# Input scaled by its inverse root once, banks emptied by ScalarE, and the keys of two heads in one unit, with the odd head's rotary product first

## What the kernel computes

```python
u = rms_norm_2(h, norm_mix_g[l])
proj = u @ w_in[l]
conv_in, c_q, c_kv, k_rope_raw, gate_logits = jnp.split(proj, cut, axis=-1)
conv_out = conformer_conv(conv_in, ...)      # a * sigmoid(gt), 31 taps, layer norm, silu, projection
mla_out = mla_attention(c_q, c_kv, ...)      # norms of both latents, 8 heads, causal softmax
gates = jax.nn.sigmoid(gate_logits).reshape(B, S, N_BRANCH, D_MODEL)
merged = gates[:, :, 0] * conv_out + gates[:, :, 1] * mla_out
h = h + merged @ w_out[l]
```

## Time and profile before

| | us |
|---|---|
| median of 3 runs (lowest to highest) | 2503.06 (2503.04 to 2503.13) |
| the profiled execution | 2503.1 |
| its span, first to last instruction | 2501.3 |
| TensorE busy | 2486.5 (99%) |
| VectorE busy | 1988.3 (79%) |
| ScalarE busy | 1244.2 (50%) |
| GpSimd busy | 305.2 (12%) |

### The profile page before, as it was taken

How to read it: one execution, slowest core, us unless ns; L and a number is a source line. 1 busy time by engine, 2 the same in 40 slices (tenths; PEclk the granted TensorE clock), 3 DMA queues, 4 the chain that set the end, 5 groups by cost and what they waited for, 6 DMA issues and landing times.

```text
span 2501.3 us, 36450 instructions
## 1 busy us (share of the span) xinstructions
PE 2486.5 (99%) x14212; PEld 2185.6 (87%) x14212; DVE 1988.3 (79%) x2830; ACT 1244.2 (50%) x1975; POOL 305.2 (12%) x250
## 2 busy tenths in 40 slices
PE   8999999999999999999999999999999999999998
PEld 7999988889999889999888899998888888888887
DVE  7878867778888688887777888876899786788873
ACT  6444444444444454444554544445577535654552
POOL 4000001220000000000023100000187221200002
PEclk9999999999999999999999999999999999999999
DMA  5333332233333323334323233334333333233331
GB/s 157 99 96 99 102 104 85 78 89 98 102 101 109 110 84 100 104 97 122 99 63 93 80 104 97 110 105 136 84 75 79 126 93 110 84 108 105 101 100 59
DMA packets 487297, 246.83 MB, mean 99 GB/s; under 512 B 42321, under 2 KB 483926, under 8 KB 486870
## 3 DMA queue, kind: packets, MB, share of 16 engines
q1 hardware_dynamic: 486674, 244.19, 33.9%
q10 hardware_dynamic: 452, 0.32, 0.0%
HBM read 240.27 MB, written 4.19 MB: 98 GB/s over the span
## 4 chain that ended last, share of the span: by engine, by line
PE 97%; DVE 1%; ACT 1%; DMA 0%; issue 0%; DVEq 0%; ACTq 0%
PE bank L893 8%; PE bank L892 8%; PE bank L891 8%; PE bank L774 6%; PE bank L775 6%; PE bank L776 6%; PE psS L913 5%; PE psS L914 4%; PE psS L915 4%; PE bank L1452 3%; PE psT L957 2%; PE psT L959 2%; PE psT L958 2%; PE psT L774 2%; PE psT L775 2%; PE psT L776 2%
## 5 line engine op out<-in xcount | busy, mean ns | idle before, releaser
L2267 DVE TENSOR_TENSOR wlo<-raw,whi 128x1024 fp32r<-128x1024 f32 (+2 forms) x212 | 288.8, 1364 | 49.8 <-ACT whi L1582 46.0
L774 PE MATMUL bank<-xhl,whi 128*128 128x512 f32 x672 | 264.5, 394 | 0.0
L775 PE MATMUL bank<-xhl,whi 128*128 128x512 f32 x672 | 261.9, 390 | 0.0
L776 PE MATMUL bank<-xhl,wlo 128*128 128x512 f32 x672 | 261.8, 390 | 0.0
L891 PE MATMUL bank<-xshl,whi 128*128 128x256 f32 x840 | 237.8, 283 | 0.0
L892 PE MATMUL bank<-xshl,whi 128*128 128x256 f32 x840 | 237.7, 283 | 0.0
L893 PE MATMUL bank<-xshl,wlo 128*128 128x256 f32 x840 | 237.7, 283 | 0.0
L1582 ACT ACTIVATE whi<-raw 128x1024 fp32r<-128x1024 f32 (+2 forms) x209 | 214.5, 1029 | 37.3 <-PE bank L776 22.2
L2330 DVE TENSOR_TENSOR wlo<-tw,whi 128x1024 fp32r<-128x1024 f32 x140 | 171.5, 1225 | 63.6 <-ACT whi L1622 63.5
L913 PE MATMUL psS<-hhi,whi 128*128 128x512 f32 x488 | 191.7, 393 | 0.0
L914 PE MATMUL psS<-hlo,whi 128*128 128x512 f32 x488 | 191.6, 393 | 0.0
(11 more groups left out here) (703 smaller groups left out, 7092.2 us busy)
## 6 DMA issues: line engine op xcount, KB each, us to landing
raw<-in_ffn_wg SPq DMA_DIRECT2D x88, 512.0 KB
raw<-in_ffn_wu SPq DMA_DIRECT2D x88, 512.0 KB
raw<-in_w_in SPq DMA_DIRECT2D x53, 512.0 KB
raw<-in_w_mlp SPq DMA_DIRECT2D x40, 512.0 KB
raw<-in_ffn_wd SPq DMA_DIRECT2D x48, 256.0 KB
raw<-in_ffn_wd SPq DMA_DIRECT2D x24, 448.0 KB
raw<-in_ffn_wd SPq DMA_DIRECT2D x48, 192.0 KB
raw<-in_ffn_wd SPq DMA_DIRECT2D x48, 128.0 KB
```

The lines of the kernel that those rows point to most:

```text
L774: pe.matmul(dest, a, rhs_hi(k), start=start and k == 0, stop=False)
L775: pe.matmul(dest, a, rhs_lo(k), start=False, stop=False)
L776: mm = pe.matmul(dest, b_, rhs_hi(k), start=False, stop=stop and k == tiles - 1)
L2267: dve.tensor_tensor(wlo[:, a:a + n], raw[:, a:a + n], whi[:, a:a + n].bitcast(F32), ALU.subtract).then_inc(s_split, 1)
```

## The change

**One scaling of the input.** As soon as the inverse root is there, GpSimd multiplies the eight chunks of x by it, into `gate_a`. When TensorE has finished a chunk of kr, ScalarE multiplies that chunk by the gain and rounds it into the old high half (`scaled_hi`), and VectorE makes the low half (`scaled_lo`). The projections a, g and gate read these, so they carry the inverse root, and their results need no product. ScalarE takes them from the banks: a copy with 0.5 for a, the tanh for g and gate (`take`). VectorE's `evict` stays for q, kv and kr alone. The addition of the squares for the key sum goes to the middle of the eight `scaled_lo`.

**Keys of two heads in one unit.** The unit of an even head holds its query and, in 128 columns, the keys of this head and the next; the odd head's unit holds a query alone. So `project(h, "k")` is made for even h only. Head parts are 640 and 384 columns wide for the split where they were 1024; the odd head's rows lie the other way round in the partitions.

**The rotary product.** In slots 4, 8 and 12 (`ROPE_FIRST`) the product of the odd head goes ahead of VectorE's taps. In slot 0 it goes behind `glu(2)`, ahead of a split.

The diff, cut to its core (renamed semaphores are left out):

```diff
+        HEAD_PARTS = [("q", 0), ("k", 0), ("k", 1), ("q", 1)]
+        HEAD_TILES = {C_IN + ORDER.index(("head", h)): QC if h % 2 else QC + KVC for h in range(H2)}
+        ROPE_FIRST = range(4, 2 * H2 - 2, 4)
...
-            in_unit("kr", 0)
+            for k in range(KC):
+                wh, wl = wcols(whi, c, k), wcols(wlo, c, k)
+                pe.matmul(bank_of[("kr", 0)], wh, chunk(xhi, k), start=k == 0, stop=False)
+                pe.matmul(bank_of[("kr", 0)], wh, chunk(xlo, k), start=False, stop=False)
+                pe.matmul(bank_of[("kr", 0)], wl, chunk(xhi, k), start=False, stop=k == KC - 1
+                          ).then_inc(s_kc if k < KC - 1 else s_used, 1)
...
-            in_unit("a", 0)
+            in_unit("a", 0, ready=lambda k: pe.wait_ge(s_xsl, k + 1))
...
-                if s % 2 == 0 and h < H2:
-                    pe.wait_ge(s_i2, evicted(*FILL[s]))
+                if s % 2 == 0 and h < H2 and h % 2 == 0:
+                    pe.wait_ge(s_ea, taken(*FILL[s]))
                     project(h, "k")
...
+            def take(kind, i):
+                act.wait_ge(s_used, unit_of(kind, i) + 1)
+                dest = {"a": tmp[i % 2][:, :], "g": tmp[2 + i % 2][:, :], "gate": gate[i]}[kind]
...
+                act.activation(dest, bank_of[(kind, i)], ACT.Copy if kind == "a" else ACT.Tanh, scale=0.5).then_inc(s_ea, 1)
+
+            def scaled_hi(k):
+                if k < KC - 1:
+                    act.wait_ge(s_kc, k + 1)
+                else:
+                    act.wait_ge(s_used, unit_of("kr", 0) + 1)
+                act.wait_ge(s_t, k + 1)
+                act.activation(chunk(xhi, k), chunk(gate_a, k), ACT.Copy,
+                               scale=gains[:, FINAL1 * KC + k:FINAL1 * KC + k + 1]).then_inc(s_xsh, 1)
...
             split(unit_of("kr", 0) + AHEAD, 0)
+            for k in range(KC):
+                scaled_hi(k)
             for j in range(QC):
                 latent_hi(j)
...
+            def scaled_lo(k):
+                dve.wait_ge(s_xsh, k + 1)
+                dve.scalar_tensor_tensor(chunk(xlo, k), chunk(gate_a, k), gains[:, FINAL1 * KC + k:FINAL1 * KC + k + 1],
+                                         chunk(xhi, k).bitcast(F32), ALU.mult, ALU.subtract).then_inc(s_xsl, 1)
...
             evict("kv", 1)
+            for k in range(KC // 2):
+                scaled_lo(k)
+            dve.wait_ge(s_lq, QC + KVC)
+            dve.tensor_tensor(chunk(lsq, QC), chunk(lsq, QC), chunk(lsq, QC + 1), ALU.add).then_inc(s_v7, 1)
+            for k in range(KC // 2, KC):
+                scaled_lo(k)
             for j in range(QC):
                 latent_norm(j)
             split(unit_of("kr", 0) + AHEAD, 0)
-            dve.wait_ge(s_lq, QC + KVC)
-            dve.tensor_tensor(chunk(lsq, QC), chunk(lsq, QC), chunk(lsq, QC + 1), ALU.add).then_inc(s_v7, 1)
             evict("kr", 0)
...
+                if s in ROPE_FIRST:
+                    head_rope(h)
+                if s % 4 == 3 and (s + 3) // 2 < H2:
+                    head_k((s + 3) // 2)
                 if s:
                     taps(DVE_SHARE.get(("slot", s), 0))
...
-                if s not in (0, 2, 4, 6):
-                    evict(*FILL[s])
...
                 if s % 2 == 0 and h < H2:
-                    if s != 2:
+                    if s > 2 and s not in ROPE_FIRST:
                         head_rope(h)
...
+            pool.wait_ge(s_inv, FINAL1 + 1)
+            for k in range(KC):
+                pool.tensor_tensor(chunk(gate_a, k), chunk(x, k), inv[:, :], ALU.mult).then_inc(s_t, 1)
```

More of the change, by code:

```diff
@@ L386, in build @@
         h_q = sem("head_q_projected")
+        s_kw = sem("second_key_weights_landed")
         s_xn = sem("squares7_added")
@@ L474, in build @@
             ORDER += [FILL[s]] + ([("head", s // 2 + 1)] if s % 2 == 0 and s // 2 + 1 < H2 else [])
-        EVICT = [e for e in ORDER if e[0] not in ("head", "v")]
+        EVICT = [e for e in ORDER if e[0] in ("q", "kv", "kr")]
+        TAKEN = [e for e in ORDER if e[0] in ("a", "g", "gate")]
         C_MRG = C_IN + len(ORDER)
@@ L1130, in project @@
                     mm = pe.matmul(dest, wl, chunk(lath, l0 + k), start=False, stop=k == n - 1)
-                mm.then_inc(h_q if part == "q" else s_used, 1)
+                mm.then_inc(h_q if part == "q" and h % 2 == 0 else s_used, 1)
             def mla_scores(s):
@@ L1919, in head_k @@
             def head_k(h):
[L1920 to L1922 removed]
+                bb, rows = h % 2 * S, head_rows(h)[0]
+                act.wait_ge(s_used, unit_of("head", h - h % 2) + 1)
+                if h >= 2:
+                    act.wait_ge(a_sc, ATT1 + 2 * h - 2)
+                act.activation(k2h[rows, bb:bb + S], bank_of[("hk", h - h % 2)][rows, :], ACT.Copy).then_inc(h_hi, 1)
             split(unit_of("q", 2) + AHEAD, 0)
@@ L1943, in _ @@
                 latent_hi(j)
+            take("a", 0)
             split(unit_of("g", 0) + AHEAD, 0)
-            glu_tanh(0)
+            take("g", 0)
             act.wait_ge(s_fr, 5)
@@ L1948, in _ @@
             split(unit_of("a", 1) + AHEAD, 0)
+            take("a", 1)
             split(unit_of("g", 1) + AHEAD, 0)
-            glu_tanh(1)
+            take("g", 1)
             split(unit_of("v", 0) + AHEAD, 0)
@@ L1965, in _ @@
             products(ADD_SHARE[("a", 2)])
+            take("a", 2)
             split(unit_of("g", 2) + AHEAD, 0)
-            glu_tanh(2)
+            take("g", 2)
             products(ADD_SHARE[("g", 2)])
@@ L1973, in _ @@
                 some = min(share, 1)
+                left = share
                 split(unit_of(*FILL[s]) + AHEAD, 0)
-                if s:
+                if s > 1:
                     products(some)
+                    left -= some
                 if s < MLA_STEPS:
@@ L1988, in _ @@
                 products(some)
-                if s >= 3:
-                    i = s - 3
-                    act.wait_ge(s_i2, evicted("gate", i))
-                    act.activation(gate[i], gate[i], ACT.Tanh, scale=0.5).then_inc(s_gt, 1)
-                elif s == 2:
-                    glu_tanh(3)
+                left -= some
                 if s:
                     products(some)
+                    left -= some
+                if s < LN_Y:
+                    take(*FILL[s])
                 if s == LN_VAR:
@@ L2010, in _ @@
                         act.activation(chunk(chi, i), chunk(zc, i), ACT.Copy).then_inc(s_ch, 1)
+                if s >= LN_Y:
+                    take(*FILL[s])
                 if s >= 2:
@@ L2023, in _ @@
                     act.activation(pt2h[:, :], psT[:, 0:(TB + 1) * P], ACT.Copy).then_inc(a_th, 1)
-                products(share - (3 * some if s else 1))
-                if s % 2 == 0 and h < H2:
+                products(left)
+                if s % 2 == 0 and h < H2 and h % 2 == 0:
                     head_k(h)
-            i = 2 * KC - 1
-            act.wait_ge(s_i2, evicted("gate", i))
-            act.activation(gate[i], gate[i], ACT.Tanh, scale=0.5).then_inc(s_gt, 1)
             for m in range(KC):
@@ L2851, in _ @@
                     glu(2)
+                    head_rope(h)
+                    split(unit_of(*FILL[s]) + AHEAD, 0)
                 if s == 2:
@@ L2857, in _ @@
                     head_rope(h)
-                if s in (4, 6):
-                    evict(*FILL[s])
+                if s in ROPE_FIRST:
+                    head_rope(h)
+                if s % 4 == 3 and (s + 3) // 2 < H2:
+                    head_k((s + 3) // 2)
                 if s:
```

222 lines of the change are left out of this document (123 added, 99 removed).

## The result

The changed kernel takes 2510.41 us in the median of 7 runs (2509.78 to 2511.66), the kernel before 2503.04 (2502.61 to 2503.13): a ratio of 1.0031, 95% interval 1.0022 to 1.0040. The forecast was 2506.5: right in direction, half the size. The profiled execution took 2509.78, its span is 2508.0 us.

What follows compares the result with a forecast made beforehand. The prediction took TensorE, busy 99% of the span, as the bound. Its terms -5.7 + 3.6 + 0.2 + 0.9 + 4.4 gave +3.4, so 2506.5 us, with a range of 2501 to 2510.5.

Steps and rivals of the forecast that it cites:

- Removed from TensorE: Heads 1, 3, 5 and 7 lose their own key projection, six matmuls each, 24 in all: -5.7 us.
- The front: At the key sum, the squares' addition comes later, behind four low halves and GpSimd's disturbance: +3.6 us (1.8 to 4.2).
- the order: At the front, four low halves, each waiting for ScalarE's high half, stand ahead of the squares' addition: +1.8 us.
- GpSimd's disturbance: At the front, GpSimd's eight products running beside VectorE make the addition later still: 1.8 us, bounded by 0 and 2.4.
- the splits between 1750 and 1763: Sign at the front: VectorE's splits there would last about 2.2 us beside GpSimd's products, against 1.22 elsewhere.
- Slots 6 and 10: Scores wait for exponentials made late by the rotary product ahead of the taps: +0.2 and +0.9 us.
- the upper bound: For slots 6 and 10, should GpSimd lengthen VectorE's split and taps: up to 1.7 and 2.4 us.
- Slot 12: The convolution's column sum waits for VectorE's sum, its taps queued behind the rotary product: +4.4 us (4.2 to 4.9).
- the clock: Rival, chance 0.12: the wait in slot 12 lowers TensorE's clock, 2 to 3 us more, 2509; the sum counted nothing.
- the sign that I had named for being wrong: One of three such signs: the granted clock falls below 1.00 between 1930 and 1950 us, around slot 12.
- contention in the slots: GpSimd lengthens VectorE's work there; with the front also at its upper end, a rival of 2508 to 2511, chance 0.20.

Runs made afterwards that it cites:

- experiment 6: Changed kernel with GpSimd's eight products replaced by writing a constant, so the scaling of the input is left out: 2508.81 us.
- experiment 3: Changed kernel with VectorE's addition of the squares ahead of all eight low halves of the scaled input instead of behind four: 2509.22 us.
- experiment 8: experiment 4's kernel with three moves: rotary product between taps and output, g 1's split ahead of the latents' norms, slot 2's taking right behind the exponentials: 2501.39 us.
- experiment 10: experiment 8's kernel with the rotated key's low halves on GpSimd, slot 0's reciprocal behind two taps, two taps in slot 4, five in slot 7: 2499.41 us.
- experiment 5: Changed kernel with sixteen more matmuls of 128x512 in slot 12, ahead of TensorE's wait for the convolution's sum: 2508.82 us.
- experiment 4: Changed kernel with the rotary product behind the taps in slots 4, 8 and 12 and the addition of squares ahead of the low halves: 2500.79 us.
- experiment 11: experiment 10's kernel with v's split earlier on both engines, slot 0's gated product ahead of its remaining taps, one tap moved to slot 8: 2498.47 us.
- experiment 1: Changed kernel with the rotary product back behind VectorE's taps in slots 4, 8 and 12: 2502.31 us, 0.9997 of before.
- experiment 2: Changed kernel with the rotary product behind the taps in slot 12 alone, still ahead in slots 4 and 8: 2504.16 us.
- experiment 9: experiment 4's kernel with 24 matmuls of 128x512 added again, six in each of slots 0, 4, 8 and 12: 2503.52 us.

## Why the forecast was half right

**Removed from TensorE:** -5.7, as measured.

**The front:** the mechanism held, addition behind four low halves that wait for ScalarE. Of the two parts of the 3.1, the order was 1.9 (forecast 1.8, where the times worked out for it, 1771.0 and 0.15 against 1769.20, also give 1.9) and GpSimd's disturbance 1.2 (1.8); experiment 6 separates them. The 1.2 did not come the way that I counted it. I expected the splits between 1750 and 1763 at about 2.2; the three take 1.22, 1.29 and 1.25, and GpSimd's products beside them take 2.28, where its first takes 1.30:

```profile
1757.46 1.29 DVE L2338 TENSOR_TENSOR wlo<-raw,whi 128x1024 fp32r<-128x1024 f32 x1
1757.62 2.28 POOL L3421 TENSOR_TENSOR gate_a<-x,inv 128x512 f32<-128x512 f32 x1
```

In these meetings the split had begun first. The two additions and the first Newton step began with a product under way, and there VectorE was the late one, as in the slowed split that I took my price from the earlier trace rows. The additions' 1.24 went into VectorE's idle time ahead of the next eviction, 1.91 before and 0.32 after:

```profile
1756.85 0.69 DVE L2757 TENSOR_TENSOR latf<-psT,inv 128x512 f32<-128x512 f32 x1 [0.32 <-PE psT L800]
```

So what reached the key sum is the Newton step's 1.1. What the prediction did not see is that the key sum only stands first in a row of late work; experiments 3, 8 and 10 moved it on to g 1, v and slot 1. VectorE's 8 us to spare of 70 were the warning: a front with so little slack hands lateness on.

**Slots 6 and 10:** mis-sized by 1.0 and 1.2. The chain was right, but I gave its operations their undisturbed durations and kept GpSimd's effect for the upper bound (1.7 and 2.4). The low half of the query took 1.78 in slots 4 and 8 where I had 0.71, and in both GpSimd had begun an addition 0.6 to 0.7 us earlier. That GpSimd is the cause there is argued from experiment 6, not tested. The likeliest case should have held one such meeting. On the way to slot 10 TensorE met the lateness in slot 9 already, at the product with the values (0.7), a place that the prediction did not list.

**Slot 12:** the wait was forecast at 4.4 and is 4.2 by starts.

**The step that failed most** is the clock, which the sum put at nothing: 2.7 us, a rival with a chance of 0.12. Its price, 2 to 3 us, was right, and the sign that I had named for being wrong, a clock below 1.00 in 1930 to 1950, came true. I argued against it from the start of the execution, where TensorE is half idle at 1.00. The runs showed instead a fall after the 4.0 us wait, and none when the wait was filled (experiment 5), and, in some executions, one after the wait of 3.2 at the front. The Trainium skill's page "TensorE: Matmul & The Clock Gate", section "Part 1: The HAM clock gate", says that an idle TensorE drops to 1.2 GHz; the trace agrees for the wait of 4.0. Clock and contention in the slots add 4.9 us to the forecast's sum; front, slot 12's wait, the small terms and the ends of the execution take 1.7 off: together the 3.2 by which the account is above the forecast.

**What the change does bring** is 2.1 us with two lines put back (experiment 4) and 4.3 with the queues ordered for it (experiment 11), of 5.7 that the matmuls are worth. The queues of experiment 11 without the rest of the change were not run; but TensorE waited only 0.2 us in this stage before, so there was hardly more for it to gain there.

## What to carry to other kernels

Ahead of an instruction that waits for the bound engine, put whatever that engine will need next: work queued behind the waiter is late by the whole wait. When time is taken off the bound engine, ask which engine feeds it with the least slack; there the gain comes back as a wait, and mending one wait shows the next. Price a forecast wait of several us on TensorE with the clock, too. And where VectorE and GpSimd meet, ask which begins first: in the front's rows the other one is late.

## What was not expected of the hardware

The same wait of 3.2 to 3.3 us at the front left the clock at 1.00 in the changed kernel's profiled execution (1765 to 1780 us) and lowered it in those of experiments 1, 2 and 5; in that of experiment 6 the clock fell after the wait of 2.1. In the profiled execution of experiment 9 even the wait of 1.8 us for g 1's split was followed by a lower clock, as it was not in those of experiments 3 and 4. That execution, 2505.01 us, is the longest of its ten (the others lie between 2503.24 and 2503.55):

```profile
1780.00:1788.00 8.00, 6.20 (x28) 4.87 (x27) 7.77 (x12) 3.69 (x7) 0.00 (x0) 1.00 0.02 6
1788.00:1794.00 6.00, 6.00 (x20) 4.74 (x20) 5.88 (x9) 5.97 (x10) 0.00 (x0) 0.72 0.33 90
```

This goes with the changed kernel's wider runs: 1.9 us from lowest to highest, where the kernel before has 0.5. What decides it in one execution stays open.
